# The address modulo 256 of four activation rows, in a transformer kernel on one core

## What is computed

```
for i in range(2):                                # first block, two layers
    sh_a, sc_a, g_a, sh_f, sc_f, g_f = split(silu(c) @ ada_w[i] + ada_b[i])
    h = rms_norm(x, norm_g[i, 0]) * (1 + sc_a) + sh_a
    y = attention(h)          # 8 heads; layer 0 plain, layer 1 differential; @ w_qkv, softmax, @ w_o
    x = x + g_a * rms_norm(y, norm_g[i, 1])
    h = rms_norm(x, norm_g[i, 2]) * (1 + sc_f) + sh_f
    g, u = split(h @ w_in, 2)                     # 1024 x 5632
    x = x + g_f * rms_norm((silu(g) * u) @ w_out, norm_g[i, 3])   # 2816 x 1024
# second block, one layer: the same frame with
#   conformer: h @ w1, gate, depthwise convolution over 31 tokens, layer norm, silu, @ w2
#   feed-forward with a depthwise convolution over 3 tokens between its two products
```

## Time and profile before

| | |
|---|---|
| median of 3 runs | 984.24 us (983.56 to 985.72) |
| profiled execution, its own time | 984.03 us |
| its span, first to last instruction | 982.2 us |
| mean granted TensorE clock | 0.993 |
| TensorE busy | 947.5 us, 96% of the span |
| VectorE busy | 820.6 us, 84% |
| ScalarE busy | 544.3 us, 55% |
| DMA, mean over the span | 238 GB/s |

### The profile page before, as it was taken

One profiled execution on the slowest core, in us unless ns is written; L12 is line 12 of the kernel. 1 busy time (PEld: TensorE's weight loads), 2 busy tenths in 40 slices (PEclk: granted clock), 3 DMA queues, 4 the chain that ended last, 5 costly groups with the idle time before them and its releaser, 6 DMA issues. The chain is left out here.

```text
span 982.2 us, 19019 instructions
## 1 busy us (share of the span) xinstructions
PE 947.5 (96%) x6806; PEld 868.6 (88%) x6806; DVE 820.6 (84%) x1217; ACT 544.3 (55%) x1023; POOL 78.0 (8%) x111
## 2 busy tenths in 40 slices
PE   4899999999999999998999999999999999999997
PEld 3899988999999888996999999989997899999996
DVE  4869988898888778777888888889998979988885
ACT  3465546454444566555554444459998555555552
POOL 2100002000000011111300000002240000000000
PEclk9899999999999999999999999999999999999999
DMA  9999983999999965652599999986340549766641
GB/s 347 328 329 349 336 278 97 349 350 343 303 333 322 279 193 162 183 174 84 166 348 359 321 322 317 318 267 173 87 129 1 181 134 301 220 196 192 190 127 43
DMA packets 240770, 234.08 MB, mean 238 GB/s; under 512 B 7497, under 2 KB 208970, under 8 KB 240714
## 3 DMA queue, kind: packets, MB, share of 16 engines
q1 hardware_dynamic: 237824, 226.52, 73.7%
q0 software_dynamic: 1616, 5.32, 1.7%
q10 hardware_dynamic: 1274, 1.52, 0.5%
HBM read 232.27 MB, written 1.06 MB: 238 GB/s over the span
## 5 line engine op out<-in xcount | busy, mean ns | idle before, releaser
L537 PE MATMUL work<-h_hi,whi_a 128*128 128x256 f32 x1360 | 379.0, 279 | 2.8 <-DVE h_lo L1412 2.8
L537 PE MATMUL work<-h_lo,whi_a 128*128 128x256 f32 x1360 | 377.4, 277 | 0.0
L537 PE MATMUL work<-h_hi,wlo_a 128*128 128x256 f32 x1360 | 377.3, 277 | 0.0
L1351 DVE TENSOR_TENSOR wlo_a<-raw,whi_a 128x1024 fp32r<-128x1024 f32 x180 | 218.6, 1223 | 52.2 <-ACT whi_a L1009 51.8
L537 PEld LDWEIGHTS work<-h_hi,whi_a 128*128 128x128 f32 x1360 | 256.3, 188 | 6.4 <-issue 2.9
L537 PEld LDWEIGHTS work<-h_lo,whi_a 128*128 128x128 f32 x1360 | 256.8, 189 | 2.7
L537 PEld LDWEIGHTS work<-h_hi,wlo_a 128*128 128x128 f32 x1360 | 256.4, 189 | 0.0
L1009 ACT ACTIVATE whi_a<-raw 128x1024 fp32r<-128x1024 f32 x180 | 187.9, 1054 | 61.1 <-PE work L537 38.3
L1361 DVE SCALAR_TENSOR_TENSOR acc<-ada_raw,csil,acc 128x1024 f32 (+1 forms) x128 | 163.5, 1279 | 7.2 <-DMA ada_raw<-in_ada_w 5.6
L1009 ACT ACTIVATE whi_b<-raw 128x1024 fp32r<-128x1024 f32 x106 | 110.7, 1055 | 81.4 <-DMA raw<-in_ffn_w_out 42.8
L1351 DVE TENSOR_TENSOR wlo_b<-raw,whi_b 128x1024 fp32r<-128x1024 f32 x106 | 128.5, 1219 | 8.8 <-ACT whi_b L1009 8.6
(11 more groups left out here) (228 smaller groups left out, 1395.6 us busy)
## 6 DMA issues: line engine op xcount, KB each, us to landing
ada_raw<-in_ada_w SPq DMA_DIRECT2D x88, 512.0 KB, 6.4
raw<-in_ffn_w_in SPq DMA_DIRECT2D x88, 512.0 KB, 7.9
ada_raw<-in_mod_w SPq DMA_DIRECT2D x48, 512.0 KB, 6.8
raw<-in_ffn_w_out SPq DMA_DIRECT2D x44, 512.0 KB, 6.2
raw<-in_f_up_w SPq DMA_DIRECT2D x44, 512.0 KB, 4.3
raw<-in_moba_w_qkv SPq DMA_DIRECT2D x24, 512.0 KB, 8.4
raw<-in_diff_w_qkv SPq DMA_DIRECT2D x24, 512.0 KB, 8.0
raw<-in_a_pw_w SPq DMA_DIRECT2D x24, 512.0 KB, 7.4
```

The source lines that it names most:

```text
L537: mm = pe.matmul(dst, w[u][:, ws], h[:, k, :], start=(k == 0 and m == 0), stop=(k == KT - 1 and m == 2))
L1351: dve.tensor_tensor(wlo[u], raw[:, u, :], whi[u].bitcast(F32), ALU.subtract).then_inc(lo[u], 1)
```

## The change

Only the list of tensors changes. `relt` (32 bytes a partition) and `ssy` (16 bytes) are moved from behind `cols` to ahead of the four rows, and one more spacer of 32 elements comes between them and the first row; the three spacers between the rows have new names. No instruction, wait or queue is touched, and no size.

```diff
         Gf = sb("Gf", [P, D])
+        relt = sb("relt", [32, H])
+        ssy = sb("ssy", [P, 2 * TT])
+        sb("spacer19", [P, 32])
         ab_hi0 = sb("ab_hi0", [P, PADW], F32R)
-        sb("spacer18", [P, 32])
+        sb("spacer21", [P, 32])
         ab_hi1 = sb("ab_hi1", [P, PADW], F32R)
-        sb("spacer20", [P, 32])
+        sb("spacer23", [P, 32])
         ab_lo0 = sb("ab_lo0", [P, PADW], F32R)
-        sb("spacer22", [P, 32])
+        sb("spacer25", [P, 32])
         ab_lo1 = sb("ab_lo1", [P, PADW], F32R)
         mix = sb("mix", [P, 2692])
         cols = sb("cols", [P, COLS])
-        relt = sb("relt", [32, H])
-        ssy = sb("ssy", [P, 2 * TT])
         taps0 = sb("taps0", [P, 72])
```

## The result

| | before | after |
|---|---|---|
| median of the runs | 984.23 us (983.56 to 985.72) | 994.31 us (993.94 to 995.62) |
| span of the profiled execution | 982.2 us | 992.6 us |

The ratio is 1.0103, 95% interval 1.0085 to 1.012. I had forecast 984.2. In the changed kernel all names stand one line lower: L537 is L538, L574 is L575, L760 is L761.

A forecast was written before the change was run, and what follows sets the result against it. TensorE's instruction spacing was taken as the bound; row matmuls, L893 and the rest sum 0 + 0 + 0, so the profiled execution stays 984.0 us and the median, 0.2 above, is forecast at 984.2, range 973 to 995.

The forecast's parts named there:

- The bound and what moves: Whole kernel: the spacing of TensorE's instructions is the time; only addresses move, and any gain or loss would pass through.
- The 984 at nothing: Matmuls with a row as stationary operand (L574, L584, L568): offset to the streaming weights goes from 64 to 0, costing nothing.
- Rival A: Row matmuls: the old offset costs and 0 is better, 226.7 ns for 233.3, -6.5 us, 977.7; chance 0.32.
- -17 and -18 us for the 984: Row matmuls, outer bounds of a gain: -17 from the skill's 216 ns, -18 from streaming alone at 215 ns.
- The untouched L537 at nothing: The 4,080 matmuls of L537: offset 64 in both kernels, so no change and no term in the sum.
- rival C: L537 behind L574: a hand-over at another moment puts blocks at 118 ns, 5.66 us; +14.3 us, 998.5; chance 0.12.
- the hand-over keeps its offset: From L574 to L537, whi_b streams while whi_a loads: address difference modulo 256 unchanged, so 113.3 ns should stay.
- Rival B: Row matmuls: at offset 0 row load and streaming weights meet more often, +9.7 ns each, 993.7 us; chance 0.14.
- L893, at nothing: Conformer taps, 312 matmuls with a row as moving operand: 113.3 to 120 ns stays, at most +-1.1 us; taken as nothing.
- ident, ones, mix, the other engines: Some 400 short matmuls, 1.8 us either side, and ScalarE and VectorE accesses lying under TensorE's work: nothing.
- The skill's rule: TensorE's two independent SBUF read ports: loading weights takes no read bandwidth from the running matmul, so no offset can matter.

The follow-up runs named there:

- experiment 1: Against the kernel before: the four rows keep their old address modulo 256, all tensors behind them lie as in the changed kernel; 984.84 us, ratio 0.9999.
- exit_h: Changed kernel, but the last two of twelve feed-forward row matmuls take a slice of h_lo (offset 64) as stationary operand; 982.78 us, 0.9982 to the kernel before.
- experiment 7: Changed kernel with the offset from streaming whi_b to loading whi_a at 192 instead of 128, other offsets kept; 994.09 us, 1.0094 to the kernel before.
- 5 and 6: h_hi and h_lo moved to 0, giving L537 offset 0, in the kernel before and in the changed one; 1006.45 us (1.0221) and 1004.36 us (1.0204).
- experiment 3: Against the kernel before: only the two low rows moved to 128 modulo 256, the high rows stay at 192; 983.83 us, ratio 0.9989.
- entry_h: Changed kernel, but the first two of twelve feed-forward row matmuls take a slice of h_hi (offset 64) as stationary operand; 996.56 us, 1.0118 to the kernel before.

## Why the prediction was wrong

**The bound and what moves: right.** TensorE's spacing was the time, and gain and loss passed through to it: +10.6 us worked out from spacings, +10.4 in the span, with the waits changed by about 1 us. I had read from the earlier trace rows that only attention and the conformer leave TensorE idle; the last feed-forward stage does too, for 6.9 of 194 us. Nothing in the sum hung on that. The addresses were right too: experiment 1 leaves only the rows.

**The 984 at nothing: a failed step, the smaller one.** I took nothing "as the rows with offsets 0, 128 and 192 are nearest". For 0 and 128 these were single matmuls at a border between two kinds, and what one takes there is not what a run of twelve takes: in the changed kernel the middle of each twelve goes at 226.6 ns at offset 0, against 233.3. Rival A named the level (226.7) and priced it at -6.5; it brought -4.3, as the first two and the last of each twelve still take about 232. By itself this step would have made the kernel faster. Of the prediction's -17 and -18 us for the 984 nothing came: the lowest steady spacing of 512 columns in any run was 226.6 ns.

**The untouched L537 at nothing: the failed step that set the sign.** The sum has no term for its 4,080 matmuls; they were to stay at 113.3 ns. Against rival C I argued that the hand-over keeps its offset "and it led to 113.3 in every step". This reason failed: with the hand-over's offset unmoved, 64 more blocks of 48 went at 117.8, 5.66 us instead of 5.45, and the level came back when only the last two row matmuls had their old offset (exit_h). Moving the hand-over's offset itself brought nothing back (experiment 7). C's mark, 5.66 after L574, was right. Its price, +14.3 against +13.6, was nearly so, in part by luck: it counts 66 entries from L574 where there are 60, three more blocks follow L555 and three steps run on L555, and of the 64 blocks that changed three lie outside feed-forward. Its mechanism, that L574 hands over at another moment, no run shows. I had also treated A and C as exclusive. The same change of the rows brought both, and the sum with both is 984.2 - 4.3 + 13.6, with 1.3 for L760 and L555, 994.8; 994.3 was measured. C with chance 0.12 was too low: the earlier trace rows showed two levels of one instruction in one trace, and the row products ahead of these blocks were what the change touched.

**Rival B** found nothing: with all twelve at offset 0, no row product became longer. Its fear came true for the other kind, in a layout that this change does not make (5 and 6).

**L893, at nothing: right.** All 312 together, waits included, took 0.4 us less. A small cost is hidden in that: the third block of taps took 4710 ns and takes 4701, but without its last spacing, which holds a wait, 4498 and 4540. **ident, ones, mix, the other engines: right**, by experiment 1 (0.9999) and VectorE's 820.6 and 821.3 us busy.

**The skill's rule.** The Trainium skill (TensorE: Matmul & The Clock Gate, Step-by-step: what each phase is for) gives TensorE two independent SBUF read ports, and I had worked out from it that no offset can matter. The runs here differ with addresses alone, from 983.8 to 1006.5 us. What the ports or banks do beneath that, no run shows.

**Open:** why and by which matmuls the row product picks the level. The trace shows starts, and a first spacing behind the row product of 0.12 in either case; it does not show the reads. Whether the very last matmul is enough, and which of the matmuls behind the first two keep L537 quick in experiment 3, was not tried. All layouts moved by multiples of 64 bytes, and that 256 is the period was not tested by itself; the two rows of j lie 1280 bytes apart, and their products took the same 2.79 us, which speaks for it.

## What to carry to other kernels

Where TensorE is full and runs in blocks of one kind, its spacing has levels a few per cent apart, which change with the operands' addresses against each other and with what ran in the block ahead. So judge a change of layout by the spacing of every kind of block, the untouched first, and price an instruction by a long run of its like, never by the one at a border; even then ask whether the run has a second level. A gain in 12 instructions that puts the 48 behind them on another level is a loss.

## What the runs showed of the hardware that I had not expected

- Spacing by offset, fp32r, means within blocks: 512 columns (L574) 226.6 ns at 0, but 232 for ten at 0 behind two at 64 in entry_h; 233.3 at 64 and 128; 229 or 233.3 at 192, product by product in turn. 256 columns (L537) 113.3 or 117.8 at 64, 117.8 at 192 (113.3 in two blocks behind taps), 118.5 to 120.0 at 128, 120.0 at 0.
- The levels pass on like a relay in attention: before, L760 behind a row product at 233.3 ns went at 113.3 in most blocks, and L537 behind it at 117.8; after, L760 went at 117.8 in seven of eight blocks, and L537 behind these at 113.3 in five of them. So in attention the change cost far less for each block than in feed-forward.
- 60 matmuls of 64 columns cost 0.11 us each, nearly the 0.118 of a matmul of 256 columns in the same block.
